# Latent attention: query rotation and two weight parts on GpSimd, two key-value copies on VectorE, two key copies on ScalarE

## What is computed

```
c_q, c_kv, k_r, qm = split(h @ w_in)            # 256, 128, 32, 256 columns
c_q, c_kv = rms_norm(c_q), rms_norm(c_kv)
q  = (c_q @ w_uq).reshape(256, 6, 96)           # the last 32 of 96 are rotated
kv = (c_kv @ w_ukv).reshape(256, 6, 64 + 128)   # key part, value
k  = concat(kv[..., :64], rotate(k_r))          # the rotated part is shared by the heads
tok = softmax(q k^T * 96**-0.5) v
mem_out = softmax(qm mk^T * 64**-0.5) mv        # four heads over 256 memory rows
x = x + rms_norm(concat(tok, mem_out) @ w_o)
```

## Time and profile before

| what | value |
|---|---|
| median of three runs | 1902.8 us |
| time of the profiled execution | 1902.97 us |
| its span | 1901.1 us |
| TensorE matmul busy | 1891.9 us (100%) |
| VectorE busy | 1285.9 us (68%) |
| ScalarE busy | 1015.4 us (53%) |
| GpSimd busy | 187.2 us (10%) |
| high half of a full slot on ScalarE, mean | 1.902 us |
| low half of a full slot on VectorE, mean | 2.288 us |

### The profile page before, as it was taken

One profiled execution on the slowest core, in us unless ns is written; L12 is line 12 of the kernel. 1 busy time (PEld: TensorE's weight loads), 2 busy tenths in 40 slices (PEclk: granted clock), 3 DMA queues, 4 the chain that ended last, 5 costly groups with the idle time before them and its releaser, 6 DMA issues.

```text
span 1901.1 us, 27792 instructions
## 1 busy us (share of the span) xinstructions
PE 1891.9 (100%) x10665; PEld 1649.2 (87%) x10665; DVE 1285.9 (68%) x1330; ACT 1015.4 (53%) x1182; POOL 187.2 (10%) x162
## 2 busy tenths in 40 slices
PE   9999999999999999999999999999999999999998
PEld 8888899888888888888888889988888888988887
DVE  5866766766666678766676666776667666666665
ACT  5544574544454557644454446564455455655453
POOL 2800122100010001100010001210001000221000
PEclk9999999999999999999999999999999999999999
DMA  8655654655665543565566566465656556546552
GB/s 299 224 187 186 198 172 140 202 188 185 199 202 196 185 150 137 189 202 187 185 207 196 192 190 194 134 208 182 199 177 206 189 182 199 189 144 195 192 186 101
DMA packets 262278, 355.27 MB, mean 187 GB/s; under 512 B 9025, under 2 KB 230721, under 8 KB 262210
## 3 DMA queue, kind: packets, MB, share of 16 engines
q1 hardware_dynamic: 258754, 341.76, 55.1%
q0 software_dynamic: 3456, 12.58, 1.9%
HBM read 353.27 MB, written 1.05 MB: 186 GB/s over the span
## 4 chain that ended last, share of the span: by engine, by line
PE 98%; ACT 1%; issue 1%; DVE 0%; POOL 0%; DVEq 0%; POOLq 0%; ACTq 0%
PE down L596 30%; PE gate_banks L471 15%; PE up_banks L471 14%; PE gate_banks L476 8%; PE up_banks L476 7%; PE up_banks L538 5%; PE up_banks L455 4%; PE up_banks L456 3%; PE up_banks L457 3%; PE up_banks L544 2%; PE gate_banks L636 1%; PE up_banks L486 0%; PE up_banks L488 0%; PE up_banks L487 0%; PE down L954 0%
## 5 line engine op out<-in xcount | busy, mean ns | idle before, releaser
L1526 DVE TENSOR_TENSOR w_lo<-raw,w_hi 128x2048 fp32r<-128x2048 f32 x309 | 706.1, 2288 | 290.1 <-ACT w_hi L1091 290.0
L1091 ACT ACTIVATE w_hi<-raw 128x2048 fp32r<-128x2048 f32 (+1 forms) x320 | 608.7, 1902 | 212.8 <-PE down L596 177.2
L471 PE MATMUL gate_banks<-h_both,w_hi 128*128 128x512 f32 x1280 | 305.8, 391 | 0.0
L471 PEld LDWEIGHTS gate_banks<-h_both,w_hi 128*128 128x128 f32 x1280 | 235.8, 188 | 45.8
L471 PE MATMUL up_banks<-h_both,w_hi 128*128 128x512 f32 x1152 | 273.9, 390 | 0.0
L596 PE MATMUL down<-w_hi,m_hi 128*128 128x512 f32 x832 | 269.2, 395 | 0.2 <-issue 0.2
L596 PE MATMUL down<-w_lo,m_hi 128*128 128x512 f32 x832 | 265.7, 390 | 0.0
L596 PE MATMUL down<-w_hi,m_lo 128*128 128x512 f32 x832 | 265.3, 390 | 0.0
L471 PEld LDWEIGHTS up_banks<-h_both,w_hi 128*128 128x128 f32 x1152 | 215.8, 188 | 44.6
L596 PEld LDWEIGHTS down<-w_hi,m_lo 128*128 128x128 f32 x832 | 156.3, 188 | 33.2
L596 PEld LDWEIGHTS down<-w_lo,m_hi 128*128 128x128 f32 x832 | 156.4, 188 | 32.9
(11 more groups left out here) (248 smaller groups left out, 2112.1 us busy)
## 6 DMA issues: line engine op xcount, KB each, us to landing
raw<-in_ffn_w_gu SPq DMA_DIRECT2D x88, 1024.0 KB, 5.1
raw<-in_ffn_w_down SPq DMA_DIRECT2D x88, 1024.0 KB, 4.9
raw<-in_ffn_w_gate SPq DMA_DIRECT2D x44, 1024.0 KB, 5.3
raw<-in_ffn_w_up SPq DMA_DIRECT2D x44, 1024.0 KB, 5.3
raw<-in_w_in SPq DMA_DIRECT2D x20, 1024.0 KB, 5.7
raw<-in_ret_w_in SPq DMA_DIRECT2D x13, 1024.0 KB, 5.3
raw<-in_w_o SPq DMA_DIRECT2D x8, 1024.0 KB, 5.0
raw<-in_w_out SPq DMA_DIRECT2D x8, 1024.0 KB, 4.9
```

Source lines behind the costliest of these rows:

```text
L471: mm(banks[:, j * 2 * S:(j + 1) * 2 * S], w_hi[:, r, c:c + P], h_both[:, k, :, :].rearrange("p a b -> p (a b)"), start=(k == 0), stop=(k = ...
L1091: act_fn(w_hi[:, r, 0:width], raw[:, r, 0:width], ACT.Copy).then_inc(hi_ready, 1)
L1526: v.tensor_tensor(w_lo[:, r, 0:width], raw[:, r, 0:width], w_hi[:, r, 0:width].bitcast(f32), ALU.subtract).then_inc(lo_ready, 1)
```

## The change

Five things are moved, all within the latent attention:

- The rotation of the queries goes from VectorE to GpSimd, with the same twelve operations and a semaphore of its own, `q_rot`; TensorE's first group of transposes waits for both row tiles of it.
- Part 5's low half goes from VectorE to GpSimd, behind the rotation, and part 6's high half from ScalarE to GpSimd, behind that. GpSimd then makes part 5's high half, the rotation, part 5's low half and part 6's high half, in this order. VectorE waits for part 5's low half ahead of its softmax steps, and ScalarE for part 6's high half.
- Key-value parts 2 and 3 are copied out by VectorE in place of ScalarE.
- The second and third turned key group are copied by ScalarE in place of VectorE.
- The scores of the second pair of memory heads move on TensorE from ahead of the key-value parts to behind their part 1, and on ScalarE the first two memory heads' exponentials alternate with the query copies of the two row tiles.

```diff
 # TensorE
                     last.then_inc(slot_done, 1)
-                    mem_step(mem, 2)
...
                         if i == 1:
+                            mem_step(mem, 2)
                             pe.wait_ge(uq_out, 4)
                             mem_step(mem, 3)
...
                         if i == 0:
-                            pe.wait_ge(qk_ready, 1)
+                            pe.wait_ge(q_rot, 2)
...
                         if i == 3:
                             mem_step(mem, 6)
-                            pe.wait_ge(qk_ready, 2)
+                            pe.wait_ge(qk_ready, 1)
...
-                    pe.wait_ge(q_T, 3)
-                    pe.wait_ge(k_T, 3)
+                    pe.wait_ge(q_T, 5)
 # ScalarE
-                        mem_step(mem, 0)
                         half = HEADS_M * QKW // 2
-                        sc.wait_ge(slot_done, b + 4)
                         for t in range(T):
+                            head_exp(mem[t])
+                            sc.wait_ge(slot_done, b + 4)
                             for c in range(2):
                                 act_fn(q_nat[:, t, c * half:(c + 1) * half], uq_banks[2 * t + c][:, 0:half], ACT.Copy).then_inc(uq_out, 1)
...
                         prob_copy(mem[1])
-                        kv_out(2)
                         head_exp(mem[2])
-                        kv_out(3)
                         head_exp(mem[3])
+                        sc.wait_ge(ukv_out, 4)
                         kv_out(4)
...
-                        sc.wait_ge(hi_ready, b + 6)
-                        high(b + 6)
+                        q_copy(4)
+                        q_copy(5)
+                        sc.wait_ge(hi_ready, b + 7)
 # VectorE
-                        for t in range(T):
-                            ve.wait_ge(uq_out, 2 * t + 2)
-                            q = q_nat[:, t, :].rearrange("p (h d) -> p h d", h=HEADS_M)
-                            rotate(q[:, :, NOPE:NOPE + 16], q[:, :, NOPE + 16:QKW], t, HEADS_M)
-                        v.tensor_copy(k_nat[:, 0, 0:1], q_nat[:, 0, 0:1]).then_inc(qk_ready, 1)
+                        third = HEADS_M * (NOPE + DV) // 3
+                        ve.wait_ge(ukv_out, 2)
+                        for i in (2, 3):
+                            ve.wait_ge(ukv_mm, i + 1)
+                            v.tensor_copy(kv_nat[:, i // 3, (i % 3) * third:(i % 3 + 1) * third], gemm_bank[i % 2][:, 0:third]).then_inc(ukv_out, 1)
...
-                        low(b + 5)
-                        for i in range(3):
-                            ve.wait_ge(qk_turned, i + 4)
-                            v.tensor_copy(mk2_T[0:QKW, 2 * i:2 * i + 2, :], qk_banks[3 + i][0:QKW, :].rearrange("p (a b) -> p a b", a=2)).then_inc(k_T, 1)
+                        ve.wait_ge(qk_turned, 4)
+                        v.tensor_copy(mk2_T[0:QKW, 0:2, :], qk_banks[3][0:QKW, :].rearrange("p (a b) -> p a b", a=2)).then_inc(k_T, 1)
                         mem_step(mem, 7)
+                        ve.wait_ge(lo_ready, b + 6)
 # GpSimd
+                    high(first_slot[u] + 5)
+                    def rotate(x1, x2, t):
+                        tmp = [rt[:, j, :].rearrange("p (a b) -> p a b", a=HEADS_M) for j in range(4)]
+                        at = S + 16 * t
+                        c = trig[:, 0:1, at:at + 16].broadcast_to([P, HEADS_M, 16])
+                        s = trig[:, 1:2, at:at + 16].broadcast_to([P, HEADS_M, 16])
+                        g.tensor_tensor(tmp[0], x1, c, ALU.mult)
+                        g.tensor_tensor(tmp[1], x2, s, ALU.mult)
+                        g.tensor_tensor(tmp[2], x1, s, ALU.mult)
+                        link(g.tensor_tensor(tmp[3], x2, c, ALU.mult))
+                        g.tensor_tensor(x1, tmp[0], tmp[1], ALU.subtract)
+                        g.tensor_tensor(x2, tmp[2], tmp[3], ALU.add).then_inc(q_rot, 1)
+                    gp.wait_ge(c_xn, T)
+                    for t in range(T):
+                        gp.wait_ge(uq_out, 2 * t + 2)
+                        q = q_nat[:, t, :].rearrange("p (h d) -> p h d", h=HEADS_M)
+                        rotate(q[:, :, NOPE:NOPE + 16], q[:, :, NOPE + 16:QKW], t)
+                        gp.wait_ge(q_rot, t + 1)
                     n = first_slot[u] + 5
+                    gp.wait_ge(hi_ready, n + 1)
+                    gp.wait_ge(lo_ready, n)
+                    g.tensor_tensor(w_lo[:, n % RING, :], raw[:, n % RING, :], w_hi[:, n % RING, :].bitcast(f32), ALU.subtract).then_inc(lo_ready, 1)
+                    high(n + 1)
```

More of the change, by code:

```diff
@@ L254, in build @@
         c_turned, c_hi_done, c_lo_done = sem("c_turned"), sem("c_hi_done"), sem("c_lo_done")
+        q_rot = sem("q_rot")
         uq_mm, uq_out, ukv_mm, ukv_out = sem("uq_mm"), sem("uq_out"), sem("ukv_mm"), sem("ukv_out")
@@ L1420, in q_copy @@
                             sc.wait_ge(qk_turned, i + 1)
-                            act_fn(mq_T[0:QKW, 2 * i:2 * i + 2, :], qk_banks[i][0:QKW, :].rearrange("p (a b) -> p a b", a=2), ACT.Copy).then_inc(q_T, 1)
+                            act_fn((mq_T if i < 3 else mk2_T)[0:QKW, 2 * (i % 3):2 * (i % 3) + 2, :], qk_banks[i][0:QKW, :].rearrange("p (a b) -> p a b", a=2), ACT.Copy).then_inc(q_T, 1)
                         kv_out(0)
@@ L1919, in _ @@
                             mem_step(mem, i)
-                        for t in range(T):
-                            ve.wait_ge(uq_out, 2 * t + 2)
-                            q = q_nat[:, t, :].rearrange("p (h d) -> p h d", h=HEADS_M)
-                            rotate(q[:, :, NOPE:NOPE + 16], q[:, :, NOPE + 16:QKW], t, HEADS_M)
-                        v.tensor_copy(k_nat[:, 0, 0:1], q_nat[:, 0, 0:1]).then_inc(qk_ready, 1)
+                        third = HEADS_M * (NOPE + DV) // 3
[3 more added lines that the diff above has]
+                            v.tensor_copy(kv_nat[:, i // 3, (i % 3) * third:(i % 3 + 1) * third], gemm_bank[i % 2][:, 0:third]).then_inc(ukv_out, 1)
                         mem_step(mem, 4)
                         ve.wait_ge(ukv_out, 6)
-                        ve.wait_ge(qk_ready, 1)
                         for t in range(T):
@@ L2074, in low_first_half, with high @@
                 g.tensor_tensor(w_lo[:, r, h], raw[:, r, h], w_hi[:, r, h].bitcast(f32), ALU.subtract).then_inc(low_begun, 1)
+            def high(n):
+                gp.wait_ge(raw_in[n % RING], 16 * (n // RING + 1))
+                gp.wait_ge(slot_done, n - RING + 1)
+                gp.wait_ge(hi_ready, n)
+                g.tensor_copy(w_hi[:, n % RING, :], raw[:, n % RING, :]).then_inc(hi_ready, 1)
             def gain_row(u, i):
```

## The result

Nine runs of the changed kernel gave a median of 1908.39 us (1907.13 to 1908.59), nine of the kernel before beside them 1902.55. The ratio is 1.0028, with a 95% interval of 1.002 to 1.0037: slower by 5 to 6 us, with the interval reaching from 4 to 7. One execution each of e1, e2, e7 and e9, and one of the kernel before beside e1 to e4, took over 8% longer than the rest; the ratios leave it out, and without it these five medians are 1902.71, 1906.48, 1902.24, 1905.86 and 1902.79. The profiled execution took 1908.39 us, its span is 1906.5.

A forecast was written before the change was run, and what follows sets the result against it. TensorE was taken as the bound, with only 1.8 us idle in the stretch. Late turning of the last memory head's probabilities makes it resume 4.8 us late, less 0.3 of vanished idles: +4.5, 1907.3 us; range 1902.0 to 1908.8.

The forecast's parts named there:

- Queries copied out: Before the key-value parts, TensorE waits some 0.6 us for the first query copy; the step costs about 0.5 us.
- Rotation: Twelve query rotation steps on GpSimd, 0.38 us each, done by 736.6; TensorE wants them at 738.09, 1.5 us of cover.
- Part 5 and part 6: Weight work on GpSimd: low half 4.6 us from 736.7, high half 2.27 us behind it; both covered for their readers.
- What stands: VectorE's normalising of the fourth memory head stands beside GpSimd's two long operations; its turning comes 5.2 us later.
- From there all is as now.: After TensorE resumes 4.8 us late, later work runs as before, less 0.3 for two vanished idles: +4.5 us.
- The key copies: If VectorE's four key copies were held instead of the normalising, they end at 746.3; the same +4.5 less 0.3.
- Rival (a): GpSimd's one-input high half does not hold VectorE, or the second normalising gets in first; +2.2, 1905.0 us; chance 0.18.
- Rival (b): GpSimd's long subtraction is cut in between or yields, so no hold matters; 1902.2 us, not slower; chance 0.18.
- (c): GpSimd's rotation steps exceed 0.65 us and queries reach TensorE late; +1.9 at 0.75 us, +8 at 1.288; chance 0.13.
- no gain of 3.8 us: Over the stretch, a gain above 3.8 us has no source, idle being only 1.8 us; chance of such gain 0.02.

The follow-up runs named there:

- e1: Changed kernel with one wait added, so GpSimd begins part 5's low half and part 6's high half only once VectorE has assembled the keys; 1902.81 us, ratio 1.000.
- e2: Changed kernel with part 6's high half back on ScalarE, part 5's low half still on GpSimd; 1906.53 us, ratio 1.0018.
- e7: e1 with the second memory scores and first exponentials back in the order of the kernel before; 1902.32 us, ratio 0.9997.
- e9: e2 with 8 extra 512-column matmuls in TensorE's wait; 1905.89 us, ratio 1.0016.
- e4: Changed kernel with part 5's low half back on VectorE and part 6's high half back on ScalarE; 1902.78 us, ratio 0.9999.
- e5: Changed kernel with 15 extra 512-column matmuls in TensorE's wait, their result overwritten; 1906.58 us, ratio 1.002.
- e8: Changed kernel with GpSimd's two weight operations begun only when the last memory head is normalised, beside VectorE's key copies; 1909.71 us, ratio 1.0037.
- e3: Changed kernel with part 5's low half back on VectorE, part 6's high half still on GpSimd; 1902.64 us, ratio 0.9999.
- e6: Changed kernel with part 5's low half on GpSimd cut into four operations of 512 columns; 1906.42 us, ratio 1.0021.

## Why the prediction was right, and where it was not

The time lies in the range, the sign and the size are right (+4.5 forecast for the median, +5.8 measured), and the reason given is the one that the runs show: e1 takes away the coincidence alone and the loss with it. By its steps:

- **Queries copied out.** Right: idle of 0.59 us before part 0 (forecast 0.6), and the shorter wait at the transposes gives it back: 0.21 instead of 0.78.
- **Rotation.** 0.40 us each (0.38 forecast, from two larger shapes). From the first start at 730.85 to the subtraction's at 735.57 are 4.7 us, 5.4 were forecast: steps overlap to 0.35 and a5's normalising cost it next to nothing (one step of 0.43; it was VectorE's pair that stood, 0.87 us for 0.62). So the long work began 0.7 us early.
- **Part 5 and part 6.** 4.53 us for 4.6. The high half took 1.95 and not 2.27, the value from the one row of before.
- **What stands.** The forecast had a6 through and both halves of the hold on a7; on before's clock the subtraction began at 736.03 in place of 736.7, a6's normalising was issued at 736.61 and so found it running, and both halves fell on a6; a7 ran freely behind. The idle came out as 3.96 us and the turns late by 4.1, where 5.2 was forecast. That term was too large by about a microsecond.
- **"From there all is as now."** This is the step that failed. TensorE's clock fell to half during the wait, and from the turns to the output projection it took 750.62 - 742.19 = 8.43 us; with the clock kept (e9: 747.53 - 740.96) 6.57. These 1.9 us, 1.8 to 2.1 by the runs of e5, were not in the sum at all. The two errors partly cancelled: with the clock kept the changed kernel takes 1906.6, 0.7 less than forecast. That the median came out only 1.1 us from the forecast is in part luck.
- **The key copies.** The prediction said that holding them would cost "the same". e8 measured 1.3 us more than the changed kernel (1.1 when each is set beside the kernel before of its own runs), since the prediction overlooked what is queued behind the copies on VectorE.
- **Rival (a)**, that the one-input high half does not hold VectorE, was priced at 2.3 us less. It is refuted by e3 and by 740.17. Taking that operation away (e2) did save 1.9 us, because the operation does hold. **Rival (b)**, no hold, and **(c)**, slow rotation, are refuted by the profile after. That no gain of 3.8 us was to be had stands: the best version idles for 1.39 us of the 1.83.

The exclusion rule of the Trainium skill, SBUF — State Buffer, "Who interferes with whom", that whichever of the two issues first keeps the other out for its whole instruction, agrees with 736.15, 740.17, e3, e6 and e8; that VectorE's normalisings and copies ran in a two-port mode, which the rule asks for, no trace shows. The row at 50.59, in which a one-input scaling by a scalar column did not delay a two-input subtraction, remains without an explanation. The next scaling of that kind in the kernel before shows the hold the other way round: begun beside VectorE's subtraction of 53.55 to 56.94, it took 3.48 us and not 1.57.

```profile
54.88 3.48 POOL L2104 TENSOR_SCALAR big<-big,lgd 128x512 f32<-128x512 f32 x1
```

## What to carry to other kernels

As far as these runs show, moving work to an idle GpSimd is free only where VectorE has no SBUF-to-SBUF operation on the critical path in that time; look for the start of each long GpSimd operation and list what VectorE does until its end. Such a hold is no wait in the profile but a duration: compare an instruction's time with the same form elsewhere. Here one wait that starts the long operation 3.5 us later was worth 5.6 us (1908.39 against 1902.81), and shorter pieces only some of that.

## What was not expected of the hardware

- A wait of TensorE of 3.96 us ended at half clock (0.50), which lasted into five microseconds of full work and cost 1.8 to 2.1 us by e5. In e2's profile a wait of 2.33 us ended at full clock, and the clock fell 0.9 us later, for some three microseconds. Two waits of 1.9 us each left it at 1.00 in e6's profile, though not, by their mean clock of 0.998, in its other runs.
- The Trainium skill, TensorE: Matmul & The Clock Gate, "What's actually happening", describes the same two levels and a fall after idling; that a wait of 2.33 us can be followed by one is what e2's trace shows.
- GpSimd's 2048-element copy took 2.27 us at 724.74 but 1.89 to 2.02 behind the rotation (in the changed kernel, e1, e3, e5, e6, e7 and e8). What makes the difference was not tried.
